# VectorE's attention steps moved ahead of the weight split of the piece that their input follows

## The reference

```
proj = h @ w_in                                  # pool, attention, conv, gates
y_pool = multiscale_pool(pool_u) * silu(pool_z)
# attention: 16 query heads, 4 key/value heads of 64, chunks of 64 tokens,
# each chunk sees itself and the two before; a sink logit for each head
s = q . k * 64**-0.5, masked
m = max(max(s), sink);  p = exp(s - m)
o = (p / (sum(p) + exp(sink - m))) . v
y_attn = o * silu(attn_z)
y_conv = conformer_conv(conv_a, conv_b) * silu(conv_z)    # depthwise, 31 taps
merged = sum over branches of sigmoid(gates_b) * (y_b @ w_branch_b)
x = x + gate * (merged @ w_out);  out = rms_norm(x)
```

## Time and profile before

| what | value |
|---|---|
| median of 3 runs | 1021.48 us (1018.66 to 1022.21) |
| time of the profiled execution | 1021.49 us |
| its span (first to last instruction) | 1019.7 us |
| PE busy | 971.0 us, 95% of the span |
| DVE busy | 673.6 us, 66% |
| ACT busy | 411.3 us, 40% |
| mean DMA rate | 216 GB/s |

### The profile page before, as it was taken

The page is one execution under the profiler, slowest core; times in us unless marked ns, Lnnn a source line. Parts: engine busy times, 40 slices in busy tenths (PEclk is TensorE's granted clock), DMA queues, the critical chain, the costliest instruction groups (busy, mean ns, idle before and its releaser), DMA issues.

```text
span 1019.7 us, 10210 instructions
## 1 busy us (share of the span) xinstructions
PE 971.0 (95%) x4227; PEld 755.6 (74%) x4227; DVE 673.6 (66%) x775; ACT 411.3 (40%) x363; POOL 9.8 (1%) x27
## 2 busy tenths in 40 slices
PE   4879999999999999999998999999999999999996
PEld 1124567888888888888887777888888888887885
DVE  3656674767858877876765644368657889766463
ACT  4131244343344334344355434435643333444432
POOL 2000000000000000000000000000000000000000
PEclk9889999999999999999998987999999999999999
DMA  9899997565555565665553343355468998975512
GB/s 313 310 332 366 342 370 240 166 205 166 166 165 187 186 205 179 197 203 184 188 165 124 110 137 125 116 173 199 145 234 315 391 341 300 323 250 182 186 62 82
DMA packets 107758, 220.00 MB, mean 216 GB/s; under 512 B 3665, under 2 KB 3745, under 8 KB 106945
## 3 DMA queue, kind: packets, MB, share of 16 engines
q1 hardware_dynamic: 106304, 212.88, 61.2%
q0 software_dynamic: 1120, 5.43, 1.5%
q10 hardware_dynamic: 288, 1.05, 0.3%
HBM read 217.25 MB, written 2.10 MB: 215 GB/s over the span
## 4 chain that ended last, share of the span: by engine, by line
PE 83%; DVE 6%; DMA 4%; ACT 4%; issue 2%; SPq 0%; DVEq 0%; ACTq 0%
PE acc_odd L941 12%; PE acc_even L941 12%; PE acc_odd L942 12%; PE acc_odd L943 12%; PE acc_even L942 12%; PE acc_even L943 12%; DMA raw<-in_w_ada 4%; PE side_b L969 4%; ACT wh L378 2%; DVE wl L584 2%; DVE ada_sums L631 1%; PE side_a L1052 1%; ACT probs L425 1%; PE side_b L955 1%; PE side_a L955 1%
## 5 line engine op out<-in xcount | busy, mean ns | idle before, releaser
L584 DVE TENSOR_TENSOR wl<-raw,wh 128x2048 fp32r<-128x2048 f32 x152 | 347.7, 2291 | 274.5 <-ACT wh L378 274.2
L378 ACT ACTIVATE wh<-raw 128x2048 fp32r<-128x2048 f32 x152 | 290.7, 1913 | 324.1 <-PE acc_even L943 144.8
L941 PE MATMUL acc_even<-wh,act_h 128*128 128x512 f32 x480 | 192.3, 401 | 1.8 <-DVE glu_a L821 0.9
L941 PE MATMUL acc_odd<-wh,act_h 128*128 128x512 f32 x480 | 189.5, 395 | 1.5 <-DVE wl L584 1.5
L943 PE MATMUL acc_even<-wh,act_l 128*128 128x512 f32 x480 | 188.7, 393 | 0.0
L942 PE MATMUL acc_even<-wl,act_h 128*128 128x512 f32 x480 | 188.5, 393 | 0.0
L943 PE MATMUL acc_odd<-wh,act_l 128*128 128x512 f32 x480 | 187.5, 391 | 0.0
L942 PE MATMUL acc_odd<-wl,act_h 128*128 128x512 f32 x480 | 187.4, 390 | 0.0
L941 PEld LDWEIGHTS acc_even<-wh,act_h 128*128 128x128 f32 x480 | 91.3, 190 | 22.9 <-issue 1.7
L941 PEld LDWEIGHTS acc_odd<-wh,act_h 128*128 128x128 f32 x480 | 90.5, 189 | 23.2 <-issue 2.7
L943 PEld LDWEIGHTS acc_even<-wh,act_l 128*128 128x128 f32 x480 | 91.1, 190 | 19.5
(11 more groups left out here) (239 smaller groups left out, 762.7 us busy)
## 6 DMA issues: line engine op xcount, KB each, us to landing
raw<-in_w_in SPq DMA_DIRECT2D x108, 1024.0 KB, 5.1
raw<-in_w_ada SPq DMA_DIRECT2D x48, 1024.0 KB, 7.0
raw<-in_w_out SPq DMA_DIRECT2D x16, 1024.0 KB, 5.0
raw<-in_w_branch_pool SPq DMA_DIRECT2D x8, 1024.0 KB, 5.0
raw<-in_w_branch_attn SPq DMA_DIRECT2D x8, 1024.0 KB, 4.9
raw<-in_w_branch_conv SPq DMA_DIRECT2D x8, 1024.0 KB, 6.1
raw<-in_conv_pw SPq DMA_DIRECT2D x4, 1024.0 KB, 5.3
x_tok<-in_x SPq DMA_DIRECT2D x1, 2048.0 KB, 8.3
```

The lines of the kernel that those rows point to most:

```text
L378: nc.scalar.activation(wh[:, m % RING], raw[:, g % RING], ACT.Copy).then_inc(high_done, 1)
L584: nc.vector.tensor_tensor(wl[:, m % RING], raw[:, load_of(m) % RING], wh[:, m % RING].bitcast(F32), ALU.subtract).then_inc(raw_done, 1)
L941: nc.tensor.matmul(sums[:, h, :], xh, wh[:, slot, i, :], start=begin, stop=False)
```

## The change

In DVE's loop the three kinds of attention steps go from the start of iteration m to just ahead of the split at the end of iteration m - 1. `score_max(u)` was in iteration `score_step(u)` + 1 and is now in iteration `score_step(u)`, `denominators(u)` goes from + 3 to + 2, and `attend(u)` from + 4 to + 3. Each of them is so moved past one split (piece m + 3 as counted from its old iteration m); the taps that stood before that split still stand ahead of it. The order of the attention steps among themselves is the same, and the last two steps, `denominators(7)` and `attend(7)`, change their place against the `low_halves` of m = 88 too. The programs of PE, ACT, POOL and SP are the same.

```
@@ DVE loop, start of iteration m
-                for u in range(UNITS):
-                    if m == score_step(u) + 4:
-                        attend(u)
-                    if m == score_step(u) + 3:
-                        denominators(u)
-                for u in range(UNITS):
-                    if m == score_step(u) + 1:
-                        score_max(u)
@@ DVE loop, end of iteration m
                 for i in range(taps_done, taps_done + TAPS_AT.get(m, 0)):
                     conv_tap(i)
                 taps_done += TAPS_AT.get(m, 0)
+
+                for u in range(UNITS):
+                    if m == score_step(u) + 3:
+                        attend(u)
+                    if m == score_step(u) + 2:
+                        denominators(u)
+                for u in range(UNITS):
+                    if m == score_step(u):
+                        score_max(u)
                 split(m + RING)
```

## The result

The changed kernel takes 1001.95 us (median of 4 runs, 1001.50 to 1002.29), the kernel before beside it 1020.84 us (4 runs, 1018.66 to 1022.21): a ratio of 0.9826, with a 95% interval of 0.9801 to 0.9851. That is 1.7% less time, with no change (1.0) outside the interval. The forecast was 1001.2 us. The span went from 1019.7 to 1000.1 us.

A forecast was written before the change was run, and what follows sets the result against it. PE, busy 95% of the span, was taken as the bound, losing time to waits and low clock in the attention stage. Waits 9.2 plus falls 11.1 gave 20.3 us off 1021.5, so 1001.2 us, range 998.5 to 1007.5.

The forecast's parts named there:

- The four waits: Attention stage: PE's four waits for `attend`, 8.6 us in all, would all be removed.
- The chain round DVE, ACT and DVE: Attention stage: a late maximum delays ACT's exponentials and copy, then DVE's split and `attend`; PE waits, 2.41 us at the third.
- The price of the waits and of the falls: Attention stage: idle time plus 0.15 us per wait, 9.2 us, and low clock, 11.1 us; 20.3 us together.
- twins: Attention stage: same sequences of transposes, scores and one piece at full clock, pricing three falls at 3.15, 3.25 and 4.72 us.
- the second term: Attention stage: three half-clock stretches behind waits would go, gaining 11.1 us, with bounds from nothing to 11.1.
- The cost of the held split: DVE's later split in the attention stage would cost nothing, hidden by 15 us of ring room; without cover, up to 26 us.
- The rest moves up: After the attention stage, 667 to 895 us, PE has no idle time, so the whole 20.3 us gain reaches the end.
- Rival A: Attention stage: one fall of the clock or one short wait stays, 3.2 to 4.7 us more, 1004 to 1006; chance 0.13.
- Rival B: Attention stage: the clock falls whatever the waits, from the mix of work; only 9.2 us gained, 1012.3 us; chance 0.05.
- C: Attention stage: the wait is handed on to another input or a late `attend`; 1017 to 1021 us; chance 0.07.
- D: Slower: the held split comes too late for PE, beyond the ring's 15 us; for example 1027 us; chance 0.03.

The follow-up runs named there:

- the two halves of the change: Against the kernel before: only maximum and denominators moved ahead of the split, 1002.53 us; only `attend` moved ahead of it, 1001.64 us.
- the last experiment on the split: Changed kernel with idle DVE work of 9.8 us ahead of the split of piece 42 and 14.6 us ahead of that of piece 61: 1003.06 us.

## Why the prediction was right

**The four waits.** All four are gone, as worked out from the earlier trace rows. `attend(0)`, the tightest, ends at 535.98 against 538.20, a room of 2.2 us (2.0 forecast); `attend(3)` has 4.5 us (4.5 forecast). The chain round DVE, ACT and DVE was the cause, shown from both ends by the two halves of the change. What I hadn't seen is that they are each enough: the sum would have been the same for either half.

**The price of the waits and of the falls.** The stage, from the start of piece 72 to that of piece 91, took 155.4 us and now takes 135.2: 20.2 us against 20.3. The three passages with a fall got shorter by 3.12, 3.25 and 4.73 us, 11.1 in all, as priced by their twins, and 9.1 us are left for the waits (9.2 forecast). In the second term, 11.1 us of falls, the size was that of one execution. It is right for that one and for about half of the runs of before (19 of 43 had a mean clock of 0.980 or less); but whether a fall comes behind a wait of 2.4 us or more is drawn in each execution (17 of 20 in the table). With no fall in this stage the kernel before would take 1002 + 9.2 = 1011.2 us. Its 43 runs had a median of 1019.87 us and a fastest of 1013.37, so that the term was between 2 and 14 us and near 8.7 at the median, if all of the spread came from this stage; the fall at 136.0 us shows that a part doesn't. The mechanism was right; that the total came within 1 us is in part luck, since the profiled execution was one of the slower ones and so were the runs beside the result (median 1020.84). Against the median of the 43 the change gives 17.9 us. The first three runs of before, 1018.66 to 1022.21, didn't show this spread. The change takes away the draw too: the four runs of the changed kernel lie within 0.8 us.

**The cost of the held split** was nothing, as forecast. The room was given as 15 us in the attention; between dense pieces it measured about 13.5.

**The rest moves up.** From 667 to 895 us PE is busy all of 228 us at full clock, as before. The missing 0.7 us between forecast and result lies ahead of the stage: piece 72 starts 0.65 us later in the profile of after (511.84 against 511.19), where nothing was changed.

**Rival A** (a fall stays) didn't come: the profiles without a wait above 0.4 us in this stage have no fall in it. The prediction weighed it with falls "in this stage alone", which is wrong: the same trace has two more falls in its first 70 us, at 39.3 and 59.8 us. They too are among waits of PE, so they don't speak for A. The Trainium skill says ("TensorE: Matmul & The Clock Gate", "A second HAM failure mode: psum-queue depth-cycling") that short rests between groups of matmuls can be enough. For the small passages of the changed kernel's attention stage this case does not bear it out, the clock stayed at 1.00; the fall at 136.0 us, behind waits of 0.68 and 1.15 us, agrees with it. **Rival B** (the clock falls whatever the waits, from the mix of work) is wrong: with the mix unchanged and the waits gone the falls are gone, with waits put back they are back, and they come among dense pieces too. How long they last went with the place, 3.3 us among dense pieces and 3.3 to 10.2 us in the attention. **Rivals C and D** didn't come; the last experiment on the split shows from where D would have.

## What to carry to other kernels

On an engine that works strictly in program order, put a step that a bottleneck engine waits for ahead of bulk work which has slack in a ring, if its input is there at that time; then check the room of the bulk work by holding it on purpose. Don't go by the longest wait in the list (ACT's 32.8 us, which cost nothing): follow the wait of the engine that sets the end back to the first step that could have run earlier. And price a wait of TensorE above its own length. Three waits near 2.5 us cost 6.3 us each in the profiled execution of before ((7.38 + 3 x 0.15 + 11.1) / 3), and 4.6 us each over ten runs where they were put in on purpose ((1015.65 - 1001.95) / 3), with the clock behind them.

## What the runs showed of the hardware that was not expected

- Whether TensorE's granted clock falls to 1.2 GHz behind a wait isn't settled by the length of the wait: from 171 to 900 us there were falls behind 0 of 8 waits up to 1.2 us, 1 of 11 near 1.5 us, 12 of 13 near 2.5 us, 5 of 7 at 2.9 to 3.9 us. No length here is shown to be safe, since one fall at 136.0 us came behind waits of 0.68 and 1.15 us.
- How long it lasts differs: 3.3 us in all five cases in the table among dense 512-column matmuls, 3.3 to 10.2 us in the thirteen in the attention, where transposes and narrow score matmuls come next. That these matmuls are the reason wasn't tested.
- The time of one unchanged kernel spread over 12 us (1013.37 to 1025.16), with its mean clock, while the 20 runs of the four kernels without a wait above 0.4 us in the attention lie within 5 us (998.50 to 1003.40). Three runs are not enough to see such a spread.
